# Reusing one y tile in the pool layer, a later gate product and earlier splits in the last attention head

## The reference, cut to what matters

```python
def pooling_mixer(u, w_in, w_group, scale, w_out):
    xb, z = jnp.split(u @ w_in, 2, axis=-1)               # 2 x 2048 columns
    xg = xb.reshape(B, S, 4, 512)                         # four groups
    pooled = stack([causal_pool_minus_self(xg[:, :, g], w) for g, w in enumerate((2, 4, 8, 16))])
    mixed = einsum('bsgi,gio->bsgo', pooled, w_group).reshape(B, S, 2048)
    return (mixed * scale * silu(z)) @ w_out

def stick_breaking_mixer(u, w_in, w_out):
    q, k, v, z = jnp.split(u @ w_in, ...)                 # 16 heads, q and k 64 wide, v and z 128
    a = sigmoid(z_ts) * prod(1 - sigmoid(z_tj), s < j < t)   # per head, with z_ts = q.k / 8, s < t
    return ((a @ v) * silu(z)) @ w_out
```

## Time and profile before

| | |
|---|---|
| median of 3 runs | 3312.39 us (3311.53 to 3315.06) |
| the profiled execution | 3315.06 us, its span 3313.0 us |
| PE busy | 3177.2 us (96%) |
| DVE, ACT, POOL busy | 1723.6 (52%), 1047.9 (32%), 533.9 us (16%) |
| mean granted clock of PE | 0.977 of full |

### The profile page before, as it was taken

One profiled execution on the slowest core, in us unless ns is written; L12 is line 12 of the kernel. 1 busy time (PEld: TensorE's weight loads), 2 busy tenths in 40 slices (PEclk: granted clock), 3 DMA queues, 4 the chain that ended last, 5 costly groups with the idle time before them and its releaser, 6 DMA issues.

```text
span 3313.0 us, 41664 instructions
## 1 busy us (share of the span) xinstructions
PE 3177.2 (96%) x14874; PEld 2561.5 (77%) x14874; DVE 1723.6 (52%) x1984; ACT 1047.9 (32%) x1364; POOL 533.9 (16%) x1003
## 2 busy tenths in 40 slices
PE   6999999999999999998995999999979999999998
PEld 4888888868888888877854788888767788888886
DVE  4555555647767767774233555555534423333343
ACT  3212111145545545542142444444422211111112
POOL 0000000004434434440001222222202000000001
PEclk9999999999999999999997999999969999999999
DMA  3111111121111111114103111111121111111111
GB/s 87 48 45 50 44 51 44 51 76 39 45 34 48 51 35 41 51 64 159 56 14 92 36 35 35 35 35 35 36 64 45 45 48 48 44 45 50 45 51 64
DMA packets 287554, 167.30 MB, mean 50 GB/s; under 512 B 79352, under 2 KB 273912, under 8 KB 287232
## 3 DMA queue, kind: packets, MB, share of 16 engines
q1 hardware_dynamic: 287488, 166.41, 17.3%
HBM read 144.33 MB, written 22.05 MB: 50 GB/s over the span
## 4 chain that ended last, share of the span: by engine, by line
PE 91%; DVE 4%; issue 1%; ACT 1%; SPq 1%; POOL 0%; DMA 0%; DVEq 0%; ACTq 0%; POOLq 0%
PE banks L702 16%; PE banks L704 16%; PE banks L703 16%; PE banks L761 8%; PE banks L762 8%; PE banks L763 8%; PE banks L791 2%; PE banks L953 1%; PE banks L894 1%; PE banks L946 1%; PE banks L711 1%; PE banks L804 1%; PE banks L806 1%; PE banks L805 1%; PE banks L783 1%
## 5 line engine op out<-in xcount | busy, mean ns | idle before, releaser
L761 PE MATMUL banks<-state_a_hi,weights_hi 128*128 128x512 f32 x1296 | 554.5, 428 | 20.9 <-DVE conv_in L1695 13.5
L762 PE MATMUL banks<-state_a_lo,weights_hi 128*128 128x512 f32 x1296 | 513.7, 396 | 0.0
L763 PE MATMUL banks<-state_a_hi,weights_lo 128*128 128x512 f32 x1296 | 513.4, 396 | 0.0
L702 PE MATMUL banks<-state_a_hi,weights_hi 128*128 128x512 f32 x1280 | 509.0, 398 | 1.9 <-DVE state_a_lo L1759 1.9
L704 PE MATMUL banks<-state_a_hi,weights_lo 128*128 128x512 f32 x1280 | 507.1, 396 | 0.0
L703 PE MATMUL banks<-state_a_lo,weights_hi 128*128 128x512 f32 x1280 | 507.0, 396 | 0.0
L1078 ACT ACTIVATE weights_hi<-weights_raw 128x1024 fp32r<-128x1024 f32 x225 | 236.7, 1052 | 646.6 <-PE banks L704 635.7
L1415 DVE TENSOR_TENSOR weights_lo<-weights_raw,weights_hi 128x1024 fp32r<-128x1024 f32 x225 | 301.1, 1338 | 137.4 <-ACT weights_hi L1078 135.1
L761 PEld LDWEIGHTS banks<-state_a_hi,weights_hi 128*128 128x128 f32 x1296 | 246.8, 190 | 62.7 <-DVE weights_lo L1415 13.9
L763 PEld LDWEIGHTS banks<-state_a_hi,weights_lo 128*128 128x128 f32 x1296 | 244.9, 189 | 58.4
L702 PEld LDWEIGHTS banks<-state_a_hi,weights_hi 128*128 128x128 f32 x1280 | 241.1, 188 | 61.0 <-DVE state_a_lo L1759 2.3
(11 more groups left out here) (265 smaller groups left out, 4788.0 us busy)
## 6 DMA issues: line engine op xcount, KB each, us to landing
weights_raw<-in_mlp_w_dram SPq DMA_DIRECT2D x64, 512.0 KB, 3.6
weights_raw<-in_gdn_w_in_dram SPq DMA_DIRECT2D x33, 512.0 KB, 4.0
weights_raw<-in_pool_w_in_dram SPq DMA_DIRECT2D x32, 512.0 KB, 3.8
weights_raw<-in_sb_w_in_dram SPq DMA_DIRECT2D x32, 512.0 KB, 4.0
weights_raw<-in_pool_w_out_dram SPq DMA_DIRECT2D x16, 512.0 KB, 3.5
weights_raw<-in_sb_w_in_dram SPq DMA_DIRECT2D x32, 256.0 KB, 4.6
mixed_dram<-stick_gate SPq DMA_DIRECT2D x16, 512.0 KB, 3.3
weights_raw<-in_sb_w_out_dram SPq DMA_DIRECT2D x16, 512.0 KB, 4.9
```

Source lines behind the costliest of these rows:

```text
L702: pe.matmul(psum[:, bank, :], whi, hi, start=(k == 0), stop=False)
L761: pe.matmul(psum[:, bank, :], whi, hi, start=(k == 0), stop=False)
L762: pe.matmul(psum[:, bank, :], whi, lo, start=False, stop=False)
L763: last = pe.matmul(psum[:, bank, :], wlo, hi, start=False, stop=(k == KC - 1))
```

## The change

Three edits. In the pool layer rows 2 and 3 of y are no longer put into `pool_hi` and `pool_lo` at step 9 but into `yA_hi` and `yA_lo` at step 11, behind a wait for the last matmul of that step. In the attention layer `take_o(b, 0)` moves on DVE from the front of slot 6 to behind `scan`, `rest_of_weights` and the projection's work of that slot. In the last head the early splits, so far in slots 6 (two), 7, 8 (two), 10 and 11 (two), are put one in each of the slots 2, 3, 4, 5, 6, 8, 9 and 10.

```diff
-        EARLY = {6: (0, 1), 7: (2,), 8: (3, 4), 10: (5,), 11: (6, 7)}
...
                 for r in range(2):
                     for m in range(2):
-                        gemm(2, 4, lambda k, c: ((yA_hi, pool_hi)[r][:, k, c], (yA_lo, pool_lo)[r][:, k, c]), (lambda: pe.wait_ge(y_lo_done, yh.add())) if m == 0 else None)
+                        gemm(2, 4, lambda k, c: (yA_hi[:, k, c], yA_lo[:, k, c]), (lambda: pe.wait_ge(y_lo_done, yh.add())) if m == 0 else None)
...
-                    elif step == 8 or step == 9:
+                    elif step == 8 or step == 11:
                         for c in range(2):
                             act.wait_ge(y_in, yi.add())
-                            if step == 9 and c == 0:
+                            if step == 11 and c == 0:
                                 act.wait_ge(bank_full, halves.value())
-                            act.activation((yA_hi, pool_hi)[step - 8][:, c, :], gated[:, 2 * (step - 8) + c, :], ACT.Copy).then_inc(y_hi_done, 1)
+                            act.activation(yA_hi[:, c, :], gated[:, 2 * (step == 11) + c, :], ACT.Copy).then_inc(y_hi_done, 1)
...
-                    if last:
-
-                        for early in EARLY.get(n, ()):
+                    if last and n >= 2:
+
+                        early = {2: 0, 3: 1, 4: 2, 5: 3, 6: 4, 8: 5, 9: 6, 10: 7}.get(n)
+                        if early is not None:
                             act.wait_ge(y_early_back, 16 * (5 if early < 5 else KC))
                             act.activation(A_hi[:, early, :], y_early[early % 5][:, :], ACT.Copy).then_inc(y_split_hi, 1)
...
-                    if s in (8, 9):
+                    if s in (8, 11):
                         for c in range(2):
                             dve.wait_ge(y_hi_done, yhd.add())
-                            dve.tensor_tensor((yA_lo, pool_lo)[s - 8][:, c, :], gated[:, 2 * (s - 8) + c, :], (yA_hi, pool_hi)[s - 8][:, c, :].bitcast(F32),
-                                              ALU.subtract).then_inc(y_lo_done, 1)
+                            dve.tensor_tensor(yA_lo[:, c, :], gated[:, 2 * (s == 11) + c, :], yA_hi[:, c, :].bitcast(F32), ALU.subtract).then_inc(y_lo_done, 1)
...
                 for n in range(first, end):
-                    if n == 6:
-                        take_o(b, 0)
                     if n + 2 < NS or not last:
                         scan(n + 2)
                     rest_of_weights(n, b)
...
                     if n == 3:
                         split_v(b, 1)
-                    for early in EARLY.get(n, ()) if last else ():
+                    if n == 6:
+                        take_o(b, 0)
+                    early = {2: 0, 3: 1, 4: 2, 5: 3, 6: 4, 8: 5, 9: 6, 10: 7}.get(n)
+                    if last and early is not None:
                         dve.wait_ge(y_split_hi, early + 1)
                         dve.tensor_tensor(A_lo[:, early, :], y_early[early % 5][:, :], A_hi[:, early, :].bitcast(F32), ALU.subtract).then_inc(y_split_lo, 1)
```

## The result

The changed kernel takes 3350.8 us, the median of five runs (3348.36 to 3352.98), against 3313.63 us for the kernel before, also five runs (3311.53 to 3315.75). The ratio is 1.0112 with a 95% interval of 1.01 to 1.0124, so the change costs about 37 us. That lies inside the predicted range (3328 to 3353), 7.6 us above the predicted value. The profiled execution took 3352.39 us, with a span of 3350.4 us; it is 37.3 us longer than the profiled execution of the kernel before.

What follows compares the result with a forecast made beforehand. PE, busy for 96% of the span, was taken to bound the kernel. Losses of 12.1 (pool layer), 12.7 (heads) and 6 us (last head) sum to 30.8, giving 3343.2 us, 0.9% slower; range 3328 to 3353.

Steps and rivals of the forecast that it cites:

- What bounds the kernel: Whole kernel: PE is busy for 96% of the span, so a change costs time wherever it makes PE wait.
- The rival in which the scans pace the heads: Attention heads: scans hold PE, so the earlier scan saves 1.28 us in each of 15 heads; 3311 us, chance 0.05.
- the one in which DVE has room in slot 6: Attention heads: the order gives the 0.9 us back, so moving take_o costs nothing; 3330.5 us, chance 0.10.
- Part A: Pool layer: PE waits after step 11 for the late y rows, losing 3.02 us a group, 12.1 us in four.
- The rival with the clock: Pool layer: PE's clock falls after each of four waits, losing 1.7 us more each time; 3350 us, chance 0.12.
- Part B: Attention heads: 15 transposes of v wait for the later take_o, 2.40 us each less their slack; 12.7 us lost.
- Part C: Last head: ACT waits in slot 2 for the early halves' loads, delaying DVE and PE; 6 us, bounds 4.6 to 8.6.
- The steps up to the first half on DVE: Last head: loads land at 1488.2, then ACT's copy, so DVE's first early half starts at 1489.35.
- the list of DVE's work: Last head: DVE's delayed work up to the end of scan(11) ends at 1510.7 to 1512.7, against 1504.1 before.
- From the end of scan(11) to `values(2)`: Last head: two early halves and three remainders on DVE just about fit into the 4.1 us there.
- spreading could help the last head: Last head: if loads landed before slot 2, early halves would fill gaps, 7.9 us less there; 3329.3 us, chance 0.04.
- The signs named in advance: Changed profile: eight pool-layer waits, 15 before transposes of v (0.4 to 1.0 us), early copy 10 us late, values(2) 6 later.

Runs made afterwards that it cites:

- part B alone: Only take_o moved behind the scan and the remainder, against the kernel before: 3328.84 us, ratio 1.0039.
- part A alone: Only the pool-layer edit (y rows 2 and 3 split after step 11 into the yA tiles), against the kernel before: 3330.17 us, ratio 1.0045.
- part C alone: Only the last head's early halves moved to slots 2 to 6 and 8 to 10, against the kernel before: 3323.26 us, ratio 1.0024.

## Why the prediction was right, and where it was not

**What bounds the kernel: right.** PE has no slack in the two stages, so each delay beyond the slack of the engine that it now waits for came out in full. The rival in which the scans pace the heads (3311) and the one in which DVE has room in slot 6 (3330.5) are refuted by part B alone: +13.1 us in the heads' stretch, forecast 12.7.

**Part A: right in its chain, short by the clock.** PE's first matmul of step 12 at 188.84 (forecast 188.8), a wait of 2.50 (2.58), and 3.1 us lost in a group in which the clock stays (3.02). The rival with the clock was given 0.12, and four falls of 1.7. It came in two of four groups, and each fall costs 1.1, because the second wait vanishes under it. The falls are 2.2 us and the four times 3.1 are 0.3 more than forecast: 14.6 instead of 12.1. With part A alone there were three falls. The Trainium skill (TensorE: Matmul & The Clock Gate, "What's actually happening") says that an idle PE falls back to half rate; these traces agree in the direction (a granted clock of 0.52 behind the wait), but the same wait of 2.5 us brought a fall in two groups and none in the two others.

**Part B: right.** 13.2 us against 12.7, inside 9.6 to 14.4. The waits view adds up to only 10.5 over 15 waits, 0.18 us a head less than the stretch has grown. A matmul that starts after a wait doesn't overlap with the one before it. In part A's second group the wait stands in the view with 2.50 us, but the matmul starts 2.89 after the one before it instead of 0.23, so 2.66 later than it could; and the next one starts 0.31 behind it. The prediction read its loss from start to start and so had that in it.

**Part C: right in its mechanism, mis-sized.** It was taken at 6 us, with 8.6 as the upper bound, and measured 10.3 in the trace, outside its own bounds, and 9.1 in the time of part C alone. The steps up to the first half on DVE hold: forecast 1489.35, measured 1517.98 - 28.34 = 1489.64. Then come three terms. The first is the list of DVE's work. Up to the end of scan(11) it was forecast to end at 1510.7 to 1512.7 and ended at 1541.34 - 28.34 = 1513.0, which is 8.9 late. That is 0.3 past the end of the range, at which every collision is paid: four of the halves and scans that overlap a POOL instruction in the rows above took 1.82 to 2.04 us, and DVE waited twice more for a mask of POOL (0.43 and 0.57).

From the end of scan(11) to `values(2)` it was 4.7 us instead of 4.1. The prediction had DVE's own list there, two halves and three remainders, just fit into the 4.1; it took 4.7, and PE waited for its end. Before, only one half stood ahead of the last remainder. It is not the clock, whose granted mean over this stretch was 0.51 before and 0.76 now; and the kernel whose halves don't wait for loads, with the same order, has the same 4.7.

The third term is `values(2)`, which took 5.0 instead of 4.2, with most of it at 1.2 GHz (a mean granted clock of 0.54, against 0.66 before). The clock was low for 34.1 us instead of 13.7 in this head, which the prediction had weighed in part A alone. 8.9 + 0.6 + 0.8 = 10.3. The step that was most off is the choice of 6 between 4.6 and 8.6: a list that is new was given about the mean of its collisions, where DVE came out of a wait of 10 us with all of its work due at once, beside a POOL that had the same. That this is why so many of the collisions came is read from the rows; no run tests it apart.

**The sum.** 30.8 us forecast, 37.3 measured in the trace: 4.3 from part C, 2.5 from part A (2.2 of it the clock), 0.5 from part B, 0.5 ahead of the heads, and 1.3 given back by later stages. Of the 7.6 us by which the median is above the forecast these are 6.5; the other 1.1 is that the median lies 1.6 us below the profiled execution, where 2.7 was taken.

That the time lies in the range is in part luck: the prediction's own bounds end at 3348, and 3350.8 is inside only by the room left for a rival, four falls of the clock (3350), of which two came; the rest of that room was filled by part C.

That spreading could help the last head (3329.3) is refuted twice: the loads were there at 1516.89 - 28.34 = 1488.55 (forecast 1488.2), and without the wait the spread halves bring nothing.

**The signs named in advance.** The 15 waits ahead of the transposes of v (up to 0.8 us) and the early copy 10.29 us late came as told. Of the eight waits in the pool layer the view names four; the short second ones are seen only from start to start in two groups. The last `values` ended about 10 us late and not 6.

## What to carry to other kernels

Where one engine is busy throughout, price a moved instruction by the time from its start to the start of the one that needs it: new way minus slack, summed over the iterations; and take both from start to start, since the waits view shows less than is lost. Ask of an instruction that PE needs what stands ahead of it on its own in-order engine: part of it may be evictions that can't end before PE itself has. And put a wait for a transfer no earlier than the transfer lands, since all that is queued behind it comes later and at once, and here part of it collided with POOL.

## What the runs showed of the hardware

Two things came unexpected. The granted clock can fall to 1.2 GHz, for 3.4 us, behind a single wait of 2.5 us with PE busy before and after, in two or three groups of four (three of four behind waits of 2.0 us), and stays up if the wait is filled with matmuls. And a stage in which the clock falls by itself, like the end of the delta-net heads, changes its length when something small is moved or delayed ahead of it: with the same program it took from 600.4 to 615.3 us in the thirteen traces of this case, one of each kernel, the shortest with the clock low for 27.2 us and the longest for 54.6. The moment at which it begins doesn't tell which: it took 605.9 us where it began at 1823.9, 600.5 where it began 2.6 us earlier and 615.3 where it began 3.8 us later, but 604.9 where it began 3.9 later. In this kernel that puts differences of up to 10 us on changes that have nothing to do with that stage, so that a gain of that size has to be found in the stage that was changed before it is believed.
